# Row scales of four norms: roots of 128x2 values on GpSimd and a product with their diagonal, in place of roots of 128x258 values on VectorE and ScalarE

## What is computed

```
def rms_norm(x, g):
    y = x * rsqrt(mean(x * x, axis=-1) + EPS)
    return y * g

# block 1
x = x + 0.5 * swiglu_ffn(x, ffn1_norm, w_gate, w_up, w_down)      # norm 0, FFN n = 0
h = rms_norm(x, mix_norm)                                          # norm 1
... = split_columns(h @ w_in)      # attention and mLSTM mixer, added to x
x = x + 0.5 * swiglu_ffn(x, ffn2_norm, w_gate, w_up, w_down)      # norm 2, FFN n = 1
# block 2
h = rmsnorm(x, ffn1_pre_g_2)                                       # norm 3
f = swiglu(h, w_gate, w_up, w_down)                                # FFN n = 2
... mixer, memory cross attention, FFN n = 3, each with its norms
```

## Time and profile before

| | us |
|---|---|
| runs (3) | 1113.09, 1117.54, 1119.35 |
| median | 1117.54 |
| the profiled execution, its own time | 1118.05 |
| its span, first to last instruction | 1116.1 |
| busy: PE / DVE / ACT / POOL | 1103.9 / 755.8 / 565.4 / 44.6 |

### The profile page before, as it was taken

The page is one execution under the profiler, slowest core; times in us unless marked ns, Lnnn a source line. Parts: engine busy times, 40 slices in busy tenths (PEclk is TensorE's granted clock), DMA queues, the critical chain, the costliest instruction groups (busy, mean ns, idle before and its releaser), DMA issues.

```text
span 1116.1 us, 19629 instructions
## 1 busy us (share of the span) xinstructions
PE 1103.9 (99%) x8422; PEld 1044.4 (94%) x8422; DVE 755.8 (68%) x870; ACT 565.4 (51%) x744; POOL 44.6 (4%) x52
## 2 busy tenths in 40 slices
PE   8999999999999999999999999999999999999997
PEld 8999999988989999999999998889988988999986
DVE  7866655898977677665577675574958658556642
ACT  7554443667464465444355545455746546444441
POOL 0000000200000000000010000010200001000000
PEclk9999999999999999999999999999999999999999
DMA  8756556644465466655576566549347537666641
GB/s 291 265 184 210 191 172 173 215 142 131 134 187 172 150 230 207 218 190 175 154 257 232 172 225 206 174 146 331 115 132 225 171 96 219 203 203 183 193 132 38
DMA packets 112422, 207.74 MB, mean 186 GB/s; under 512 B 8912, under 2 KB 18768, under 8 KB 112208
## 3 DMA queue, kind: packets, MB, share of 16 engines
q1 hardware_dynamic: 109968, 198.53, 55.8%
q0 software_dynamic: 2080, 7.87, 2.1%
q10 hardware_dynamic: 288, 0.10, 0.0%
HBM read 205.42 MB, written 1.05 MB: 185 GB/s over the span
## 4 chain that ended last, share of the span: by engine, by line
PE 91%; DVE 5%; issue 1%; ACT 1%; DMA 1%; POOL 0%; DVEq 0%; POOLq 0%; SPq 0%; ACTq 0%
PE pair L469 89%; PE pair L473 2%; DVE w_lo L1489 1%; DMA stage<-in_ffn_w_up 1%; ACT w_hi L1074 0%; DVE work L1832 0%; DMA stage<-in_ffn_w_gate 0%; DVE top L1830 0%; DVE x L1680 0%; DVE xr L1515 0%; DVE nmax_a L1716 0%; DVE big L1710 0%; DVE ga L1734 0%; DVE dm L1861 0%; DVE r_low L1543 0%
## 5 line engine op out<-in xcount | busy, mean ns | idle before, releaser
L1489 DVE TENSOR_TENSOR w_lo<-stage,w_hi 128x1024 fp32r<-128x1024 f32 (+1 forms) x382 | 451.8, 1209 | 206.5 <-ACT w_hi L1074 205.3
L1074 ACT CAST w_hi<-stage 128x1024 fp32r<-128x1024 f32 (+1 forms) x382 | 382.8, 1030 | 232.6 <-PE pair L469 217.4
L469 PE MATMUL pair<-h_hi,w_hi 128*128 128x256 f32 x1760 | 491.7, 280 | 2.4 <-DVE w_lo L1489 2.4
L469 PE MATMUL pair<-h_hi,w_lo 128*128 128x256 f32 x1760 | 488.6, 278 | 0.0
L469 PE MATMUL pair<-h_lo,w_hi 128*128 128x256 f32 x1760 | 488.6, 278 | 0.0
L469 PEld LDWEIGHTS pair<-h_hi,w_hi 128*128 128x128 f32 x1760 | 331.2, 188 | 7.1 <-issue 5.4
L469 PEld LDWEIGHTS pair<-h_hi,w_lo 128*128 128x128 f32 x1760 | 332.7, 189 | 0.0
L469 PEld LDWEIGHTS pair<-h_lo,w_hi 128*128 128x128 f32 x1760 | 331.0, 188 | 0.2
L469 PE MATMUL pair<-f_hi,w_lo 128*128 128x256 f32 x352 | 97.2, 276 | 0.0
L469 PE MATMUL pair<-f_hi,w_hi 128*128 128x256 f32 x352 | 97.2, 276 | 0.0
L469 PE MATMUL pair<-f_lo,w_hi 128*128 128x256 f32 x352 | 97.2, 276 | 0.0
(11 more groups left out here) (314 smaller groups left out, 1136.6 us busy)
## 6 DMA issues: line engine op xcount, KB each, us to landing
stage<-in_ffn_w_down SPq DMA_DIRECT2D x88, 512.0 KB, 3.9
stage<-in_ffn_w_gate SPq DMA_DIRECT2D x85, 512.0 KB, 4.6
stage<-in_ffn_w_up SPq DMA_DIRECT2D x84, 512.0 KB, 4.6
stage<-in_w_in SPq DMA_DIRECT2D x52, 512.0 KB, 4.1
stage<-in_w_out SPq DMA_DIRECT2D x16, 512.0 KB, 4.1
stage<-in_xa_wkv SPq DMA_DIRECT2D x16, 512.0 KB, 4.8
stage<-in_xa_wq SPq DMA_DIRECT2D x8, 512.0 KB, 4.5
stage<-in_xa_wo SPq DMA_DIRECT2D x8, 512.0 KB, 4.9
```

What stands on the lines that cost most here:

```text
L469: return e.matmul(o, l, r, start=start, stop=stop, skip_group_check=True)
L1074: e.copy(m.w_hi[u % PLACES][:, plan.place(u)], m.stage[u % STAGES][:, 0:w]).then_inc(s.hi, 1)
L1489: e.tensor_tensor(m.w_lo[slot][:, plan.place(u)], m.stage[u % STAGES][:, 0:w], m.w_hi[slot][:, plan.place(u)].bitcast(F32), ALU.subtract). ...
```

## The change

For each of the four norms, `mean_squares` keeps only the two products 128x1. DVE adds EPS to 128x2 values. GpSimd raises them to the power -0.5 in two operations of 128x1 (`column_roots`) straight into columns 256 and 257 of `rB[i]`. DVE multiplies the identity matrix by them (`diagonal`, 128x256: two diagonal matrices, times D). PE multiplies `all_over_d` with that (`spread_roots`, one product 128x256), which puts the scales in a row on all partitions. ACT copies the row out of PSUM (`root_rows`). The reciprocal, the Newton step and the square root are gone.

The order is changed as well. In FFN 0 the gate block takes (4,6), (6,8) as units 8 and 9, and up takes (4,5) with SHIFT, (5,6), (6,8) as units 10 to 12; in FFN 1 and 2 the SHIFT moves from the second up unit to the first. The small products come after unit 8 in FFN 0, after F + 1 in FFN 1 and 2, after U + 2 in the mixer, and the spreading product comes one unit later in the FFNs and after U + 6 in the mixer. In the mixer DVE squares `q_raw` earlier. GpSimd's list gets the eight powers between its transfers. The first ACT function of the program is Sigmoid instead of Square; ACT's list has 9 table loads where it had 16.

```diff
-                    for k0, k1, shift in ((4, 6, 0), (6, 7, 0), (7, 8, SHIFT)):
-                        add(blocks[0], gate, 0, k0, k1, shift)
                     for k in (4, 6):
-                        add(blocks[1], up, 0, k, k + 2)
+                        add(blocks[0], gate, 0, k, k + 2)
+                    for k0, k1, shift in ((4, 5, SHIFT), (5, 6, 0), (6, 8, 0)):
+                        add(blocks[1], up, 0, k0, k1, shift)
...
-                    for k0, k1, shift in ((0, 1, 0), (1, 2, SHIFT), (2, 4, 0), (4, 6, 0), (6, 8, 0)):
+                    for k0, k1, shift in ((0, 1, SHIFT), (1, 2, 0), (2, 4, 0), (4, 6, 0), (6, 8, 0)):
...
-    return (6, 3, 3, 4)[n] if b == 0 else 4 if b < 5 else 2
+    return (5, 3, 3, 4)[n] if b == 0 else 4 if b < 5 else 2
...
# PE
         for t in range(T):
-            mm(ps[:, S + t:S + t + 1], m.ssum[:, t * P:(t + 1) * P], m.all_over_d[:, 0:1], t == 0, False)
-        ins = mm(ps[:, 0:S], m.all_over_d[:], m.ssum, False, True)
+            ins = mm(ps[:, t:t + 1], m.ssum[:, t * P:(t + 1) * P], m.all_over_d[:, 0:1], t == 0, t == T - 1)
...
+    def spread_roots(i):
+        ps = take(2)
+        e.wait_ge(s.diag, i + 1)
+        mm(ps[:, 512:512 + S], m.all_over_d[:], m.diag, True, True).then_inc(s.sprd, 1)
+        free[2] = (s.rB, i + 1)
...
-        at = 3 if n == 0 else 2
+        at = 3 if n == 0 else 1
...
+            if j == at + 1:
+                spread_roots(i)
...
# ACT
-        e.wait_ge(s.var, i + 1)
-        e.activation(m.std, m.var, ACT.Sqrt).then_inc(s.std, 1)
+        e.wait_ge(s.sprd, i + 1)
+        e.copy(m.rB[i][:, 0:S], m.pair[2][:, 512:512 + S]).then_inc(s.rB, 1)
...
# DVE
-        e.tensor_scalar(m.var, m.pair[2][:, 0:S + T], EPS, None, ALU.add).then_inc(s.var, 1)
-    def inverse_roots(i):
...
+        e.tensor_scalar(m.var, m.pair[2][:, 0:T], EPS, None, ALU.add).then_inc(s.var, 1)
+    def diagonal(i):
+        e.wait_ge(s.rcol, T * (i + 1))
+        e.scalar_tensor_tensor(m.diag, bcast(m.ident[:], 1, T), float(D), bcast(m.rB[i][:, S:S + T], 2, P), ALU.mult, ALU.mult)
...
-                lo_to(F + 6)
+                lo_to(F + (5 if n == 0 else 3))
                 variances(i)
-                inverse_roots(i)
+                lo_to(F + (6 if n == 0 else 4))
+                diagonal(i)
+                lo_to(F + (7 if n == 0 else 6))
+                e.wait_ge(s.rB, i + 1)
...
# GpSimd
+    def column_roots(i):
+        e.wait_ge(s.var, i + 1)
+        for t in range(T):
+            e.tensor_tensor(m.rB[i][:, S + t:S + t + 1], m.var[:, t:t + 1], m.half_pow[:, 0:1], ALU.pow).then_inc(s.rcol, 1)
```

More of the change, by code:

```diff
@@ L224, in __init__ @@
         self.sqT = flat(xr[:])
-        self.ssum, self.var, self.std = (self.sqT[:, 512 * p:512 * p + S + n] for p, n in ((1, 0), (2, T), (3, T)))
+        self.ssum, self.var, self.diag = (self.sqT[:, 512 * p:512 * p + n] for p, n in ((1, S), (2, T), (3, S)))
         self.xc, self.sg = (xr[:, t, :].rearrange("p (c s) -> p c s", c=4) for t in range(T))
@@ L688, in mixer1 @@
             scaled_unit(U + j, 1)
-        mean_squares(1)
+            if j == 2:
+                mean_squares(1)
         free[1] = (s.ev, 1)
@@ L692, in mixer1 @@
         free[0] = (s.ev, 2)
+        spread_roots(1)
         units(7, 9)
@@ L1143, in ffn_by_columns @@
             if b == 0:
-                hi_to(F + (8 if n == 0 else 7))
-                std_deviations((0, 2, 3)[n])
+                hi_to(F + (9 if n == 0 else 7))
+                root_rows((0, 2, 3)[n])
             hi_to(F + 8 * b + gate_units(n, b) + 5)
@@ L1247, in mixer1 @@
         rows_evac(U + 6, 0, m.kvn, nw=336)
+        root_rows(1)
         hi_to(U + 15)
@@ L1428, in scalar_program @@
     e.wait_ge(s.pow, 1)
-    e.activation(m.stat[:, 0, 0:1], m.half_pow[:, 0:1], ACT.Square)
+    e.activation(m.stat[:, 0, 0:1], m.half_pow[:, 0:1], ACT.Sigmoid)
     e.wait_ge(s.par, 16)
@@ L1734, in by_rank @@
             e.tensor_tensor(out, m.pair[pair][:, :].rearrange("p (c s) -> p c s", s=S), bcast(m.rB[1][:, 0:S], 1, 4), ALU.mult).then_inc(s.dev, 1)
+        lo_to(U + 6)
+        variances(1)
         lo_to(U + 7)
-        variances(1)
-        lo_to(U + 8)
-        inverse_roots(1)
+        diagonal(1)
+        lo_to(U + 9)
+        e.wait_ge(s.ev, 1)
+        e.tensor_tensor(m.q_nrm[:, :, 0:512], m.q_raw[:], m.q_raw[:], ALU.mult)
         lo_to(U + 11)
@@ L1769, in mixer1 @@
         lo_to(U + 15)
+        e.wait_ge(s.rB, 2)
         by_rank(0, U + 10, 1, m.iqT[:])
@@ L2190, in gpsimd_program @@
     U = plan.M1
+    column_roots(0)
     e.wait_ge(s.xT, 4)
```

28 lines of the change are left out of this document (11 added, 17 removed).

## The result

| | before | after |
|---|---|---|
| executions | 11 | 11 |
| median us | 1116.13 | 1110.29 |
| lowest to highest us | 1111.44 to 1120.16 | 1107.84 to 1112.40 |
| the profiled execution, its own time | 1118.05 | 1111.69 |
| its span | 1116.1 | 1109.9 |

The ratio of after to before is 0.9932, 95% interval 0.991 to 0.9954: the changed kernel is faster, by 5.8 us between the medians and by 5.1 to 10.0 us by the interval, where 1.0 us was forecast. The ratio is worked out over the runs side by side and is not the quotient of the two medians (0.9948). Its spread is as telling as its median. The executions before lie 8.7 us apart, those after 4.6 us.

A forecast was written before the change was run, and what follows sets the result against it. PE, busy 1103.9 of 1116.1 us, was taken as the bound. Terms of -1.37, +0.2 and +0.2 gave -0.97, say -1.0 us, hence 1116.5 us against the median of 1117.54; range 1112 to 1122 for 8 in 10.

The forecast's parts named there:

- What bounds the kernel: Whole kernel: PE, busy 1103.9 of 1116.1 us, sets the time; relieving DVE and ACT is worth nothing by itself.
- Part 1: First norm, FFN 0: the stall near 27 us goes (-1.82 us), a new wait of 0.45 comes, net -1.37 us.
- The wait for the diagonal: FFN 0, near 24 us: PE waits 0.45 us at the spreading product for GpSimd's powers and DVE's diagonal.
- The cover named for unit 12 and for `gr`: FFN 0 behind the diagonal: unit 12's low part (25.5, needed 27.7) and DVE's gate product (by 27) come in time.
- Rival B: FFN 0: GpSimd's first power is dearer, deciding from about 2.8 us; PE waits 5.0 us, 1121.1 us in all; chance 0.08.
- Part 2: PE's own work at the four norms: three products in two places instead of one, 0.05 us each, +0.2 us.
- the covers of part 3: Mixer, FFN 1 and 2: the new chain is ready before PE needs it, by 0.5 us in FFN 1; no wait added.
- rival A: Late stretches (FFN 3's spacing, half clock at 231 to 233) fall well or gain is larger: 1110.5 to 1115; chance 0.10.
- the last paragraph of part 3: Mixer and FFNs: products between small and spreading product may come at the slow spacing, 0.4 us at most, taken as +0.2.
- The prediction's last sign: Whole kernel: wrong if the difference is over 5 us either way, for which only spacing and clock are large enough.
- Rival C: FFN 0 to 2: SHIFT unit straight behind the product fails to restore fast spacing; one FFN 1120.7 to 1123.5; chance 0.14.
- Rival D: GpSimd's chain also late at FFN 1 and 2, or parts cost twice: 1117 to 1118, no change; chance 0.08.

The follow-up runs named there:

- g2: The kernel before with the change at norms 1, 2 and 3 alone, norm 0 in FFN 0 as before with its stall: 1114.68 us, ratio 0.9991.
- the cut kernel: Kernel before, changed kernel, h1 and h2, each with everything behind FFN 0 left out: mean 202.09 us for the cut kernel before, 197.47 for the cut changed kernel.
- f2: The changed kernel with the SHIFT of FFN 1 and 2 back in the second up unit: 1110.08 us, ratio 0.9939.
- g1: The kernel before with the change at norm 0 (FFN 0) alone, norms 1 to 3 as before: 1112.88 us, ratio 0.9939.
- e1: The kernel before with the low part of unit 12 made ahead of the norm's chain in FFN 0, taking out only the stall: 1115.04 us, ratio 0.9982.
- h1: The kernel before, its norm kept, with FFN 0's shifted unit moved behind the place of the stall: 1115.17 us, ratio 0.999.
- h2: The changed kernel without SHIFT in FFN 0 alone: 1114.86 us, ratio 0.9978.
- e2: The changed kernel with SHIFT = 0 everywhere: median 1116.32 us of all twelve, ratio 0.9981 from the nine under 1122 us.

## Why the prediction was wrong

It gave 1116.5 us with 1112 to 1122; the time was 1110.29. The direction was right, the size a sixth.

**What bounds the kernel** held. So did the uselessness of relieving DVE and ACT: 10.9 and 8.1 us less work, and g2 with three of the four norms gives 0.9991.

**Part 1** got its net right and its parts wrong. The wait of 1.6 us at 27 went as forecast; the two profiles differ by 1.4 us over that stretch, against 1.37. Unit 13 starts at 29.48, 2.3 us earlier than at 31.8 and not 1.2 to 1.8, since 0.8 us stood ahead of the norm already. The wait for the diagonal, 0.45 us, didn't come. Two columns took 1.46 us on GpSimd (21.23), not 2.02: the first call cost 0.9 us there and not the 1.5 that had been carried over from the power of the earlier trace rows. A wait of 0.17 us stands in its place, at 20.61, for the low part of unit 9, whose 1024 columns DVE now finishes just behind the small products. The cover named for unit 12 and for `gr` was there.

**Rival B** fell at its condition: it wanted a first call of over 2.8 us. The longest 128x1 power took 1.48 us, in the mixer, 3.6 us behind GpSimd's transfers. The Trainium skill's 6 us for freshly loaded code (GPSIMD Engine Reference, 2.1 Instruction dispatch) isn't seen at either place.

**Part 2 and the covers of part 3**, 0.2 us each: in FFN 1 and 2 the profiles differ by 0.05 us over the norm. DVE's EPS addition at FFN 1 takes 0.16 us, the diagonal starts at 382.66, and PE doesn't wait. Right, and too small to matter. (FFN 3's slow stretch is written as 102 x 0.004 = 4 us in rival A; 4 us is 102 x 0.04.)

**The failed step** is that the sum knows only PE's waits around the norm and prices everything behind them at nothing: the draws of PE's distance and of the clock, in the last paragraph of part 3 and in rival A, and the end of the kernel, for which it has no term at all. The prediction saw that PE has two distances between products, that a disturbance "leaves it to chance", and that after the stall at 29.00 it "became fast by itself". It priced the distance only for products that the change adds and for stretches that the one profile showed slow, and concluded for the rest that "nothing new lies there". The runs show three things in its place:

- The end. The store of the result takes 1.05 us less in every profile of the changed kernel. It is nearly a fifth of the gain and has nothing to do with PE.
- The stall can cost more than its length: a half clock of 1.7 us behind it in three of eight profiles, and once, in the cut kernel, a slow FFN 0 of 5.9 us. In the cut kernels this makes 0.8 and 1.2 us in the mean. The profile on which the prediction rests had drawn both well.
- The long times are gone. The fastest executions differ by 3.2 us (1111.03 of 132, 1107.84 of 23), which is little more than the stall and the end are worth; the other 2.6 us of the medians are long times that no longer come. This goes with norm 0's new form and order taken whole: after, its repetition, f2 and g1 have no time over 1115.2 in 42, while e1 without the stall and g2 have five each over 1118, and h1 with the shifted unit moved has three over 1117. Which draw it is stays open.

**Rival A** nearly had the time (1110.5 to 1115) and had the wrong places: it looked at FFN 3 and at 231 to 233. In the pair of profiles FFN 3 did gain 3.8 us, but g1 has the slow FFN 3 and keeps the gain, and the second profile of the kernel before has the fast one without it. That the pair of profiles differs by 6.2 us, near the medians' 5.8, is chance: the losses and gains behind FFN 0 happened to add up so. The prediction's last sign, that over 5 us only spacing and clock are large enough, missed the end.

**Rival C** fell. Its doubt, whether the unit works straight behind the product, is answered: with it FFN 0 is fast in every profile of the changed kernel. What it feared happens when the unit is left out, 4 of 4 in the cut kernel.

**Rival D**, no change, is excluded by the interval.

**Range.** The three times before lay 6 us apart, which the prediction took for a median's uncertainty. It was the sum of draws, of which a change of order can remove some. With 6.6 us in play in the stretch behind the changed place, the range should have reached further down.

**Still open.** The cut kernels give 4.0 us in the median and 4.6 in the mean; with the end, of which they have only 0.17 us, that is 4.9 to 5.5 of the 5.8. But the full kernels don't show it part by part. No profile of a full kernel with the stall has a slow FFN 0. e1 takes the same stall away and keeps the long times. h2 should be some 1.5 us slower than before by its cut form and its shorter end, and is 2.5 us faster (its interval ends at +0.8); h1 should be 3.5 us faster and is 1.1 (its interval reaches to 4.0). So the draws behind FFN 0 may not be independent of what happens in it; with 9 us of them in play this was not resolved. Why there are two distances is open as well: the shift of 80 floats in the weights' place bears on it, but no shift other than 0 and 80 was run. Nor is the shifted unit the whole rule. e2, which has no shift anywhere, shows a fast FFN 0 in its profile (the row stands below), while h2, without it in FFN 0 alone, shows a slow one, and so do its four cut executions by their times. In e2 PE was in the slow distance ahead of the spreading product and in the fast one from 25 us on; in h2 and its cut form it was the other way round.

```profile
40.00:180.00 140.00, 140.00 (x1237) 140.00 (x1237) 89.62 (x82) 64.30 (x69) 0.00 (x0) 1.00 0.65 202
```

## What to carry to other kernels

A stall on the engine that sets the time can have a price behind it as well as its own length: look at the granted clock and at the distance between products in the stretch that follows, in several executions and not in one. If the times of a kernel are spread over more than its profile explains, ask which long stretches may run in either of two ways, and whether the change puts a disturbance ahead of one of them or takes one away. To see such a draw, cut the kernel behind the stretch: in 200 us a step of 6 us stands out in each time, in 1116 us it is lost among three others. And lay two profiles over each other to the very end, not to the last product: two programs that store the same result in the same way can differ there, here by 1.05 us.

## What the hardware showed that was not expected

- Products of 128x256 come every 0.1133 or every 0.1178 us at a granted clock of 1.00, for 165 us on end. In the cut kernels, by the profiles and by the times of all executions, FFN 0 was slow behind the stall in one of five (in none of eight profiles of full kernels), slow behind the spreading product in four of four, and fast in nine of nine where a unit of 12 products with its weights 80 floats further stood last.
- Where the stall put the starts of two of PE's products 2.13, 2.55 and 2.21 us apart, the granted clock was at its lower level (1.2 GHz) for 3.4 us behind it; where they were 1.98 (twice), 1.93, 1.85, 1.76 or 1.65 us apart it was not. In the cut kernel before three of five executions have a mean clock that fits it.
- A mean clock below 1.00 need not cost anything: in every profile the granted clock falls to its lower level behind PE's last product, in the cut kernels for 5.2 to 7.9 us.
- A transfer of 8 KB in the queue `instruction` during the last store goes with a landing 1.1 us later (3.1 against 2.1 us).
- A GpSimd power of 128x1 takes 0.55 us when another stands right before it, 0.9 in FFN 0 as the first after 19 us of idle time, 1.48 in the mixer 3.6 us behind GpSimd's own transfers.
